# One product of probabilities and values for two token tiles, in the attention of layers 0 and 1

## The reference, cut to what matters

```
s_loc = einsum(q, k_window) * 64**-0.5      # 8 heads, 2 key/value heads, 64 wide
s_ctx = einsum(q, k_context) * 64**-0.5
p = softmax([s_loc + mask, s_ctx, sink])    # the sink takes weight and gives no value
o = p_loc @ v_window + p_ctx @ v_context    # 256 queries x 512 keys, context queries: 256 keys
```

## Time and profile before

| what | value |
|---|---|
| time, median of 3 runs | 1058.48 us (1057.12 to 1058.69) |
| span of the profiled execution | 1054.8 us |
| PE busy | 1028.3 us, 97% |
| DVE, ACT busy | 396.7 us (38%), 334.0 us (32%) |
| attention of layer 0 | from 150.4 to 247.4 us of the span |
| attention of layer 1 | from 373.4 to 419.8 us of the span |
| granted clock of PE | 1.00 in both |

### The profile page before, as it was taken

One profiled execution on the slowest core, in us unless ns is written; L12 is line 12 of the kernel. 1 busy time (PEld: TensorE's weight loads), 2 busy tenths in 40 slices (PEclk: granted clock), 3 DMA queues, 4 the chain that ended last, 5 costly groups with the idle time before them and its releaser, 6 DMA issues.

```text
span 1054.8 us, 13362 instructions
## 1 busy us (share of the span) xinstructions
PE 1028.3 (97%) x4956; PEld 661.4 (63%) x4956; DVE 396.7 (38%) x1194; ACT 334.0 (32%) x785; POOL 27.5 (3%) x96
## 2 busy tenths in 40 slices
PE   6999999999999999999999999999999999999996
PEld 2444554544466777888888457788888944444442
DVE  5438536444244756255832004841112421000004
ACT  5132134435033247245554014750101421111112
POOL 0000000000000000000000000000000010100000
PEclk9999999999999999999999999999999999999999
DMA  9972125762233331453444342139645699999996
GB/s 365 422 280 80 40 80 185 292 242 83 77 121 119 128 112 53 168 202 125 156 160 160 120 159 81 41 124 423 251 160 230 228 388 421 420 422 420 421 421 248
DMA packets 33933, 227.45 MB, mean 216 GB/s; under 512 B 4577, under 2 KB 4849, under 8 KB 8112
## 3 DMA queue, kind: packets, MB, share of 16 engines
q1 hardware_dynamic: 30784, 214.97, 52.3%
q10 hardware_dynamic: 1920, 9.80, 2.5%
q0 software_dynamic: 1168, 1.85, 0.5%
HBM read 222.15 MB, written 8.41 MB: 219 GB/s over the span
## 4 chain that ended last, share of the span: by engine, by line
PE 94%; DMA 2%; DVE 2%; ACT 1%; issue 0%; SPq 0%; DVEq 0%; ACTq 0%
PE lin L524 24%; PE aux L524 11%; PE lin L993 10%; PE lin L617 7%; PE sc L548 6%; PE aux L993 5%; PE aux L880 4%; PE sc L653 4%; PE aux L683 3%; PE sc L958 3%; PE sc L524 3%; PE lin L669 3%; DMA Y<-ada_in 2%; PE sc L753 1%; PE sc L591 1%; PE lin L753 1%
## 5 line engine op out<-in xcount | busy, mean ns | idle before, releaser
L524 PE MATMUL lin<-H,ring 128*128 128x256 f32 (+1 forms) x1104 | 264.4, 401 | 1.9 <-ACT PR L1333 1.9
L524 PEld LDWEIGHTS lin<-H,ring 128*128 128x128 f32 x1104 | 209.4, 190 | 55.6 <-issue 27.1
L524 PE MATMUL aux<-Y,ring 128*128 128x512 f32 (+1 forms) x256 | 83.1, 486 | 0.0
L617 PE MATMUL lin<-ring,H 128*128 128x384 f32 (+2 forms) x224 | 76.2, 501 | 0.0
L524 PEld LDWEIGHTS aux<-Y,ring 128*128 128x128 f32 x256 | 48.5, 190 | 33.7 <-issue 29.3
L548 PE MATMUL sc<-H,ring 128*128 128x512 f32 (+1 forms) x192 | 67.3, 496 | 0.0
L1210 ACT ACTIVATE SP<-lin 128x512 f32<-128x512 f32 (+2 forms) x88 | 42.1, 486 | 72.1 <-PE lin L669 71.9
L1726 DVE SCALAR_TENSOR_TENSOR UN<-UN,cols 128x512 f32<-128x512 f32 (+1 forms) x120 | 64.5, 610 | 0.0
L617 PEld LDWEIGHTS lin<-ring,H 128*128 128x128 f32 x224 | 40.8, 193 | 34.9 <-issue 22.4
L1221 ACT ACTIVATE SP<-SP,ST 128x513 f32<-128x513 f32 (+4 forms) x88 | 53.8, 612 | 6.6 <-DVE ST L1653 6.4
L548 PEld LDWEIGHTS sc<-H,ring 128*128 128x128 f32 x192 | 34.8, 189 | 30.3 <-issue 25.6
(11 more groups left out here) (335 smaller groups left out, 1210.0 us busy)
## 6 DMA issues: line engine op xcount, KB each, us to landing
ring<-w_stream SPq DMA_DIRECT2D x119, 1024.0 KB, 4.9
SP<-w_stream SPq DMA_DIRECT2D x13, 1024.0 KB, 20.7
UN<-w_stream SPq DMA_DIRECT2D x10, 1024.0 KB, 19.6
PR<-w_stream SPq DMA_DIRECT2D x8, 1024.0 KB, 21.8
CW<-w_stream SPq DMA_DIRECT2D x8, 1024.0 KB, 21.8
X<-w_stream SPq DMA_DIRECT2D x8, 1024.0 KB, 23.7
Y<-w_stream SPq DMA_DIRECT2D x8, 1024.0 KB, 18.3
PR<-ada_in SPq DMA_DIRECT2D x5, 1024.0 KB, 26.9
```

The costliest lines, as they stand in the source:

```text
L524: m = mm(dst, w[:, k, :], rhs(k), start=n == 0, stop=n == KT - 1)
L617: m = mm(bank[:, 0:width], src[:, k, tt * P:(tt + 1) * P], w[k // 4][:, k % 4, 0:width], start=k == 0, stop=k == KT - 1)
```

## The change

The two pairs 2n and 2n + 1 of the same heads share their weights (V does not depend on the token tile). Their value products are made together: 256 columns of two PT buffers, which lie two apart in the ring of six, go through the same weights. `turned(g)` gives the two buffers as one operand; where the ring wraps around, the step between them is negative. The products stand at the even steps: pairs 0 and 1 at step 4, pairs 2 and 3 at step 6, and so on to pairs n_pairs - 2 and n_pairs - 1 at step n_pairs + 2. DVE copies 256 columns at once. The two modulation turns go from filling pieces 13 and 25 to 15 and 27, so from steps 6 and 12 to 7 and 13, and DVE's loops for them from 7 and 13 to 8 and 14. The attention of the third block (abm) is as it was.

```diff
-ADA_TURNS = {13: 1, 25: 2}
+ADA_TURNS = {15: 1, 27: 2}
...
-                                              YB[:, j, s, c]))
+                                              both=YB[:, j, s, :]))
...
-            if step == n_pairs + lag:
-                return [n_pairs - 1]
-            return [q for q in (step - lag - 2, step - lag - 1) if 0 <= q < n_pairs - 1] if (step - lag) % 2 else []
+            return [step - lag - 2] if step - lag > 0 and (step - lag) % 2 == 0 else []
+
+        def turned(g):
+
+            a, b = g % TURNED, (g + 2) % TURNED
+            return PT[:, a:b + 1:2, :] if a < b else PT[:, a::b - a, :]
...
+                        if name != "abm":
+                            pair, g = items[a:a + 2], first[name] + a
+                            pe.wait_ge(lin_taken, T_LAST[g + 3] + 1)
+                            V_TURN.update((g + x, at["aux"]) for x in range(4))
+                            bank, nk = aux_bank(), len(pair[0]["vs"])
+                            for j in range(nk):
+                                for x in range(2):
+                                    m = mm(bank[HALVES[x], 0:SEQ], pair[x]["vs"][j], turned(g + x)[:, :, j * P:(j + 1) * P],
+                                           start=j == 0, stop=j == nk - 1)
+                            m.then_inc(aux_ready, 1)
+                            continue
...
-                        it = items[2 * q]
-                        v.tensor_copy(it["to"], take()[:, 0:it["to"].shape[-1]]).then_inc(aux_taken, 1)
+                        to = items[2 * q]["to"] if name == "abm" else items[2 * q]["both"]
+                        v.tensor_copy(to, take()[:, 0:to.shape[-1]]).then_inc(aux_taken, 1)
```

More of the change, by code:

```diff
@@ L390, in GT, with item @@
             return H[:, 1, 2 + n, :] if n < 6 else Y[:, 6 + n, :] if n < EARLY else PR[:, n, :]
-        def item(q, ks, mask, vs, bank, scale, sink=None, to=None, qs=None):
-            return dict(qs=qs or [q], ks=ks, mask=mask, vs=vs, bank=bank, scale=scale, sink=sink, to=to,
+        def item(q, ks, mask, vs, bank, scale, sink=None, to=None, qs=None, both=None):
+            return dict(qs=qs or [q], ks=ks, mask=mask, vs=vs, bank=bank, scale=scale, sink=sink, to=to, both=both,
                         w=sum(k.shape[-1] for k in ks))
```

## The result

The changed kernel takes 1060.28 us (median of 20 runs, 1058.21 to 1062.36) against 1058.61 (20 runs, 1056.95 to 1059.21) for the kernel before. The ratio is 1.0021, with a 95% interval of 1.0015 to 1.0028: slower by 0.21%, at the edge of the 0.2% that I had called no change; the interval leaves out 1. The forecast was 1060.1.

The account below looks back on a forecast made before the run. The prediction took PE, busy for 97% of the span, as the bound. Layer 0's 0.25 us and layer 1's 1.35 us added 1.6 to 1058.5, giving 1060.1 us, range 1057.0 to 1062.5.

Parts of the forecast that it names:

- Part 1: Value products of both layers: merged, two pairs take 1.89 us against 1.90 before; 0.2 us saved in all.
- Part 2: DVE's copies: 24 of 128 columns become 12 of 256, each 0.28 to 0.56 us; counts for nothing mid-stage.
- Part 3: Layer 1's attention: PE idles 1.0 us in step 5, last two pairs wait behind ACT's last copy; costs 1.35 us.
- Part 4: Layer 0's attention end: the 0.61 us wait on DVE goes, ACT's last copy comes later; costs 0.25 us.
- Part 5: Moved modulation turns: PE's four transposes go one step on, DVE's additions one loop on; nothing counted.
- The sum: Whole kernel: 0.25 + 1.35 = +1.6 us, so 1060.1 us, 0.15% slower.
- B: Rival: the negative step between two PT buffers halves the moving stream's pace, 5.2 us more, 1065.3 us; chance 0.06.
- E: Rival: weight loads take PE time and half of them go, saving 4.4 us, 1055.7 us; chance 0.10.
- D: Rival: unseen slack in DVE's read or ACT's chain, nothing lost, -0.5 to +0.5, 1058.5 us; chance 0.19.
- C: Rival: ACT's last chains follow PE's delay fully, 2.0 us in layer 1, 0.7 in layer 0, 1061.2; chance 0.17.

Follow-up runs that it names:

- narrow: The changed kernel with each merged value product made as two of 128 columns, 320 matmul records instead of 160; 1058.88 us, ratio to before 1.0013.
- apart_l1: The changed kernel with the last two pairs valued apart in layer 1 alone; 1059.41 us, ratio to before 1.0014.
- piece5: The changed kernel with one filling gate piece of layer 1 moved from step 6 to step 5; 1059.30 us, ratio to before 1.0016.

## Why the prediction was right, point by point

**Part 1, the products: right.** 1.88 us against the 1.89 I had, and 1.01 against 1.02; all widths and the negative step cost what the columns cost. Narrow gave 0.19 us for what had been reckoned at 0.2.

**Part 2, DVE's copies: right.** One of 256 columns takes 0.42 us, between 0.28 and 0.56, and PE waits for none.

**Part 3, layer 1: right in both waits, a little too large.** The turn of pair 5 came 37.83 us after the first scores against 36.23 before, so the 1.6 us of the forecast. DVE's read ended 2.87 us after the start of the scores, as before. The wait for it shows as 0.85 us, reckoned at 1.0, only because the turn ahead of it, with nothing behind it, takes 1.04 us in the chain in place of 0.87; from scores to scores step 5 takes 2.93 us, reckoned at 2.97. ACT's row began 1.3 us later, as forecast, but ended only 1.06 later, counted from the first scores: I had taken it as without a hole, and before it had two small ones, 0.14 us ahead of the copy of the gate piece and 0.12 ahead of that of pair 6, as both PE products came late; now they came in time. The wait of 0.4 us that I had put ahead of the turn of pair 6 was under 0.1: I had let it wait for the scaling of both items, and the turn starts when the first is scaled (`probs_scaled`, item by item). I had also given that turn 0.5 us where 8 transposes take 0.87; it touched nothing, as ACT was behind it. Together 1.09 in place of 1.35.

**Part 4, layer 0: right in its mechanism.** The wait on DVE's copy went, one of 1.08 us on ACT's copy came, the sum was +0.14 where I had +0.25. Most of this difference is no finding: I had set the end, 247.57, against the start in the timeline, 247.35, and not against that in the chain, 247.42, from which it is 0.15. Within it two small things cancel. As in layer 1 ACT's row was pushed less than PE's work ahead of it: 0.34 at its first copy in place of 0.4, and 0.28 at its last; and the last value product took 1.08 us in place of 1.02.

**Part 5: right.** The turns at L604 moved by a step and nothing waits for them.

**The sum** was 1.6 us, and the stages gave 1.23. The measured ratio is worth 2.2 (1.6 to 3.0), the difference of the medians 1.67. What the forecast lacked is the clock, which costs some runs 1.7 us and others twice that. An estimate from the groups: 12 of 20 runs of before had one low stretch, that is 1.0 us on average; of the changed kernel 10 had one and 5 had two, 1.7 us on average. Those 0.7 us and the 1.23 of the stages make 1.9. So the mechanism was right, and it is luck that the time was met to 0.2 us: the stages were 0.4 too large, and the clock, which the forecast left out, went the other way.

**The rivals.** B (the negative step) and E (the weight loads) are refuted by the traces of the changed kernel and of narrow. D (nothing lost) is out by the two waits. C had ACT follow fully: it followed less than in the forecast itself. That the median came out 0.8 us below C's 1061.2 is no evidence against it, with steps of 1.7 us between runs; the stages are.

## What to carry to other kernels

Before two narrow products are joined into a wide one, look at the distance from start to start: where it already goes with the columns (here 0.110 us for 128 against 0.217 for 256), joining saves next to nothing, and only the new places of the work count. Work without any dependence on its step is cover; when half of the steps lose it, compare the step's remaining length with the latency of the round trip through the other engines (here 2.9 us from the start of the scores to the end of DVE's read), and move filling work to the steps that fall short. At the end of a stage keep one independent product between the last turn and the last product: it was worth 0.85 us in layer 1.

## What was not expected of the hardware

In the trace of apart_l1 the granted clock fell to 1.2 GHz for 3.4 us behind waits of PE of 0.90 and 1.08 us with 0.69 us of work between them; in the 7 us up to 247 us of the span PE was busy for 5.02. It happened in one of the traces with these two waits and not in the five others (the three of the changed kernel, narrow and piece5), and the changed kernel's trace has the same 5.02 us with the clock at 1.00 throughout.
